# The expert down matrix read as four neighbouring rows per partition, with SwiGLU transposes that take every fourth column

## What is computed

```python
def moe_swiglu(h, w_router, w_gate, w_up, w_down):
    probs = jax.nn.softmax((h @ w_router).astype(jnp.float32), axis=-1)
    top_p, top_i = lax.top_k(probs, TOP_K)
    top_p = top_p / jnp.sum(top_p, axis=-1, keepdims=True)
    gates = jnp.sum(jax.nn.one_hot(top_i, N_EXPERTS, dtype=jnp.float32) * top_p[..., None], axis=-2)
    y = jnp.zeros(h.shape, jnp.float32)
    for e in range(N_EXPERTS):
        y = y + gates[..., e:e + 1] * swiglu(h, w_gate[e], w_up[e], w_down[e]).astype(jnp.float32)
    return y.astype(h.dtype)
```

## Time and profile before

| what | value |
|---|---|
| time, median of 3 runs | 1859.83 us (1857.74 to 1859.93) |
| the profiled execution, its time | 1861.72 us |
| the profiled execution, its span | 1860.0 us |
| PE busy | 1790.0 us, 96% of the span |
| DVE busy | 1168.1 us, 63% |
| ACT busy | 885.7 us, 48% |
| read from HBM | 429.82 MB |

### The profile page before, as it was taken

One profiled execution on the slowest core, in us unless ns is written; L12 is line 12 of the kernel. 1 busy time (PEld: TensorE's weight loads), 2 busy tenths in 40 slices (PEclk: granted clock), 3 DMA queues, 4 the chain that ended last, 5 costly groups with the idle time before them and its releaser, 6 DMA issues.

```text
span 1860.0 us, 27046 instructions
## 1 busy us (share of the span) xinstructions
PE 1790.0 (96%) x10718; PEld 1447.5 (78%) x10718; DVE 1168.1 (63%) x1128; ACT 885.7 (48%) x926; POOL 31.2 (2%) x93
## 2 busy tenths in 40 slices
PE   7989999999999999979999999999999999999997
PEld 6757788888767799658888878878788888788785
DVE  4660100000057674658988878888789888788885
ACT  2351110000014322256676667677666766676673
POOL 5000000000010000000000000000000000000000
PEclk9998999999999999979999999999999999999998
DMA  9201333334323100429999989999899999899992
GB/s 323 91 9 40 130 135 135 135 108 141 96 91 136 46 4 4 170 91 347 370 340 347 361 307 356 354 353 360 306 358 362 344 344 365 304 363 351 349 365 111
DMA packets 190894, 432.62 MB, mean 233 GB/s; under 512 B 9587, under 2 KB 10611, under 8 KB 190772
## 3 DMA queue, kind: packets, MB, share of 16 engines
q1 hardware_dynamic: 190384, 430.76, 64.1%
q10 hardware_dynamic: 388, 0.14, 0.0%
HBM read 429.82 MB, written 1.05 MB: 232 GB/s over the span
## 4 chain that ended last, share of the span: by engine, by line
PE 85%; DVE 8%; ACT 4%; issue 2%; ACTq 0%; DVEq 0%
PE ps L974 15%; PE ps L976 15%; PE ps L975 15%; PE ps L640 11%; PE ps L651 6%; PE ps L676 2%; PE ps L552 2%; PE ps L941 2%; PE ps L956 2%; PE ps L624 2%; DVE wsplit L1704 2%; PE ps L896 1%; PE ps L795 1%; PE ps L810 1%; PE ps L997 1%
## 5 line engine op out<-in xcount | busy, mean ns | idle before, releaser
L1704 DVE TENSOR_TENSOR wsplit<-raw_w,wsplit 128x2048 fp32r<-128x2048 f32 x336 | 749.8, 2284 | 68.4 <-ACT wsplit L1288 68.4
L1288 ACT ACTIVATE wsplit<-raw_w 128x2048 fp32r<-128x2048 f32 x336 | 624.1, 1914 | 63.8 <-PE ps L976 63.8
L974 PE MATMUL ps<-wsplit,xsplit 128*128 128x512 f32 x896 | 361.2, 403 | 8.7 <-DVE wsplit L1704 8.1
L976 PE MATMUL ps<-wsplit,xsplit 128*128 128x512 f32 x896 | 351.3, 392 | 0.0
L975 PE MATMUL ps<-wsplit,xsplit 128*128 128x512 f32 x896 | 350.9, 392 | 0.0
L640 PE MATMUL ps<-arena 128*128 128x272 f32 x896 | 208.8, 395 | 3.6 <-DVE arena L1352 3.6
L974 PEld LDWEIGHTS ps<-wsplit,xsplit 128*128 128x128 f32 x896 | 169.3, 189 | 47.9 <-DVE wsplit L1704 12.7
L640 PEld LDWEIGHTS ps<-arena 128*128 128x128 f32 x896 | 171.2, 191 | 41.1 <-issue 4.0
L976 PEld LDWEIGHTS ps<-wsplit,xsplit 128*128 128x128 f32 x896 | 169.4, 189 | 36.6
L975 PEld LDWEIGHTS ps<-wsplit,xsplit 128*128 128x128 f32 x896 | 169.8, 189 | 35.2 <-issue 1.9
L974 PE MATMUL ps<-wsplit,hsplit 128*128 128x512 f32 x448 | 179.6, 401 | 0.0
(11 more groups left out here) (305 smaller groups left out, 1657.2 us busy)
## 6 DMA issues: line engine op xcount, KB each, us to landing
raw_w<-in_moe_w_gate SPq DMA_DIRECT2D x114, 1024.0 KB, 6.5
raw_w<-in_moe_w_up SPq DMA_DIRECT2D x112, 1024.0 KB, 7.6
raw_w<-in_moe_w_down SPq DMA_DIRECT2D x112, 1024.0 KB, 6.9
arena<-in_ffn_w_gate SPq DMA_DIRECT2D x7, 2048.0 KB, 7.8
arena<-in_ffn_w_up SPq DMA_DIRECT2D x7, 2048.0 KB, 7.7
arena<-in_ffn_w_down SPq DMA_DIRECT2D x8, 1792.0 KB, 7.7
arena<-in_attn_w_qkv SPq DMA_DIRECT2D x3, 2048.0 KB, 12.7
arena<-in_attn_w_o SPq DMA_DIRECT2D x2, 2048.0 KB, 20.6
```

What stands on the lines that cost most here:

```text
L974: mm(o, x_[0], w_[0], start=first_, stop=False)
L976: return mm(o, x_[1], w_[0], start=False, stop=last_)
L1288: A(wsplit[:, m % NRING, 0, :], raw_w[:, m % NRAW, :], ACT.Copy).then_inc(w_hi, 1)
L1704: v.tensor_tensor(wsplit[:, m % NRING, 1, :], raw_w[:, m % NRAW, :], wsplit[:, m % NRING, 0, :].bitcast(F32), ALU.subtract).then_inc(w_lo, 1)
```

## The change

In L369 the split of the 512 rows of a down block changes from (k p) to (p k). Partition `p` now holds the four neighbouring rows `4 p` to `4 p + 3`, and chunk `k` holds row `4 p + k`. Half `h` of a down tile is the chunks `2 h` and `2 h + 1` as before, which are now the rows `4 p + 2 h` and `4 p + 2 h + 1`: for each partition 8192 bytes that lie in one piece in HBM. Before they were two pieces of 4096 bytes, 512 KB apart. The pieces of neighbouring partitions start 16384 bytes apart now; the rows between them are those of the other half. The issuing instruction changes its form from 128x2x1024 elements to 128x2048.

To match, the `k`-th transpose takes the columns `k`, `k + 4`, `k + 8` and so on of the 512 hidden columns: 128 words that lie 16 bytes apart in a partition, in place of 128 words in one piece. All else stays, instruction for instruction and in the same order on every engine: the writing side of the transposes, `hsplit`, the matmuls, the waits and the rings.

```diff
@@ -366,7 +366,7 @@
 
             we_g = moe_w_gate[0].rearrange("e (k p) n -> e p k n", p=P)
             we_u = moe_w_up[0].rearrange("e (k p) n -> e p k n", p=P)
-            we_d = moe_w_down[0].rearrange("e (f k p) n -> e f p k n", p=P, k=QB)
+            we_d = moe_w_down[0].rearrange("e (f p k) n -> e f p k n", p=P, k=QB)
 
             def expert_tiles(i, it, a, b):
 
@@ -994,7 +994,7 @@
                         if q in (0, XQ):
                             pe.wait_ge(xg_ev, tables * 2 + (2 if q == 0 else 4))
                         for k in range(QB):
-                            last = tr(ps[:, 4, k * P:(k + 1) * P], hbuf[:, q % 2, k * P:(k + 1) * P], ident[:, :])
+                            last = tr(ps[:, 4, k * P:(k + 1) * P], hbuf[:, q % 2, :].rearrange("p (i k) -> p k i", k=QB)[:, k, :], ident[:, :])
                         last.then_inc(et_mm, 1)
 
                     def down(q):
```

## The result

| | median us | lowest to highest | runs |
|---|---|---|---|
| before | 1859.95 | 1857.74 to 1864.69 | 14 |
| after | 1863.94 | 1858.44 to 1866.93 | 14 |

The ratio is 1.0023 with a 95% interval of 1.0014 to 1.0032: 4.3 us slower, 2.6 to 6.0. The time lies in the range of the prediction, 3.6 us above its likeliest value. The forecast was "no change", with a bound of 0.2%. The ratio lies on that bound and the interval reaches to both sides of it, so what can be said is: slower by a little, at or just past what the prediction still called no change. The median also lies 0.9 us above the range of 1857 to 1863 us that the prediction gave to its own forecast.

A forecast was written before the change was run, and what follows sets the result against it. The prediction took PE to bound the expert stage. DMAs 0, transposes 0 to 0.8 us and PE's waits unchanged gave 1861.7 to 1862.5 us profiled, 1860.3 us on the runs' scale; range 1856 to 1881 us for 8 in 10.

The forecast's parts named there:

- no change: Whole kernel: time within 0.2% (3.7 us) of before, likeliest 1860.3 us, own range 1857 to 1863; chance 0.55.
- What bounds the kernel: Expert stage: PE is the bound, holding 85% of the span; no engine is released by a weight half's landing.
- The down DMAs at zero: The 112 down DMAs: 8 KB pieces in place of 4 KB change the time by 0.
- their margin: Down halves: 17 us spare per turn, 0.6 us each, so hidden until one takes 3.3 us and not 2.7.
- The second rival: Down DMAs get slower and the DMA becomes the bound; at 3.6 us per half 34 us more, 1894 us; chance 0.05.
- The streaming side as the bound of a plain transpose: Transposes, L997: streaming the identity sets 107.5 of 109 ns; the load's 49 ns of reading is hidden, 60 ns to spare.
- f: Transposes' loads, L997: factor by which the 16-byte stride lengthens the reading part; costs little up to 2, loads bound above 2.2.
- the 111.6 ns that the prediction took from the gather: Pace of L941, whose load is 192 ns; taken as the most a transpose would need at a doubled reading part.
- The factor of the stride: Transposes, L997: the reading part grows at most twofold, so the 224 transposes cost 0 to 0.8 us.
- the marks that the prediction named: Load of L997 in the changed profile: 139 ns unchanged, up to 192 if reading doubles, above 220 the prediction is wrong.
- The first rival: Strided loads become the bound at L997 alone, three exposed per block: 7 us to 15 to 20 us slower; chance 0.34.
- Nobody amplifies it: Engines waiting for the transposes, mainly ACT (20.5 us): they lose nothing against PE, so the price is paid once, on PE.

## Why the prediction was right or wrong

**What bounds the kernel: right.** PE's stream is the bound, and nothing of the 8 KB pieces shows in the time: alone they gave 0.9997 (0.9989 to 1.0006).

**The down DMAs at zero: right, but their margin was mis-sized.** The prediction divided by a turn of 244 us. A turn is 255 us, by the first matmuls of two turns shown above (1078.17 and 1333.34). With 255 us the margin is 28 us per turn, 1.0 us per down half, and the point 3.7 us in place of 3.3. The run with 512 B pieces, at some 3.6 us, already cost PE 4.4 us at three places. So an average over the turn says roughly where the price begins, and not that nothing is paid before. The second rival was still weaker than I put it: the transfers did not get slower either, 6.9 us to landing against 7.0.

**The streaming side as the bound of a plain transpose: right.** The load went from 139 to 187 ns at a stride of 8 and the pace stayed at 109 ns. The point at which a strided load begins to cost, a reading of some 107 ns, f of 2.2, holds within a few ns. By the same sum the load at 8 has a reading of 97 ns and costs nothing. The load at 16 (196 ns) has 106 ns and a pace of some 112 ns, like the 111.6 ns that the prediction took from the gather.

**The factor of the stride: this step failed.** I took f up to 2. A strided load occupies 120 ns, against the 49 ns that I had worked out for the reading: f is about 2.4. The record says the same: 208 ns less 139 is 69 ns more, 118 ns of reading. It passes the 109 ns of the streaming side by 11 ns, and the term that was put at 0 to 0.8 us measured 2.4 us. My reason, that the streaming side takes 2.2 words per ns, was of words in one piece, as the text granted, and did not carry over. The load's record of 208 ns is just between the marks that the prediction named (192 for f = 2, 220 as the sign of error), and the block's 0.47 us just above "0.43 to 0.45".

**The first rival: right in mechanism and place, below its prices.** The strided load became the bound, at L997 alone. Three steps of a block are exposed, as many as it said, but they are the third and fourth transpose and the matmul behind them, 11 ns each, with some 10 ns more around them: 2.4 us and not 7 to 20. It had 0.34; it is what happened. That the forecast "no change" and the likeliest time came out so near all the same is owed to the small size of the excess, 11 ns, and not to the reason that was given for f.

**Nobody amplifies it: right.** ACT's wait for the transposes went from 20.5 to 21.2 us, and PE's waits did not change.

**The Trainium skill's rule.** "SBUF — State Buffer", section "Door 1: The DMA port swizzle", says that two hits on a 16-byte line are needed for full bandwidth. The load did slow, as the rule says. But a stride of 2 words has two words on each line and had the same 120 ns as 4, and a stride of 8 was cheaper than both. The measurements decide: the rule gives the sign here, but not which stride is cheap.

**What stays open.** The paces and the turns show 2.4 us. The medians say 4.3 (2.6 to 6.0), 3.5 (1.5 to 5.6) and, with the stride alone, 3.0 us (1.1 to 4.8). Two of the three intervals hold 2.4, and the first just misses it. The granted clock may carry the rest. Its mean was 0.9785 over the 29 runs of the kernel before, 0.9778 with the stride alone and 0.9773 with both, and among those 29 runs 0.001 less clock goes with some 1.2 us more. That would be 0.7 and 1.3 us, which with 2.4 gives 3.1 and 3.7 us. It is a relation between runs and no experiment. Whether the stride makes the falls of the clock more frequent, or whether the runs happened to lie that way, is not shown; the kernel in which DVE makes the order, without a strided load, had 0.9773 too.

## What to carry to other kernels

Before a DMA is improved, look whether any engine is released by its landing: here a DMA share of 0.95 left room for down halves to grow from 2.7 to 3.0 us at no price, and larger pieces gave nothing back. When a single time seems unchanged, compare the waits of PE and the granted clock as well: the 512 B pieces cost 4.4 us of waits that a better clock covered. Before an operand is given a stride, find out which side of the instruction sets its pace and how far the other is from it; a load that grows by 69 ns cost 11 ns, and one that grows by 48 cost nothing. A new order that is put into an access pattern adds no instruction, but can be paid by the engine that walks it, here by PE (2.4 us) or, when moved, by DVE and through it again by PE (2.8 us).

## What the runs showed of the hardware

- The load of a transpose of 128 x 128 float32 words takes 139 ns in one piece, 187 ns at a stride of 8 words, and 209 ns at 2 and 4 words. The price does not grow with the distance, and 6 words was the dearest of those tried (137 ns for a transpose, against 109 in one piece).
- DVE's product of 128 x 512 float32 took 679 ns written in one piece and 1105 ns with neighbouring words written 128 words apart and all operands walked as 128 x 4.
- DMA packets of 8 KB for a third of the traffic made the others' time to landing longer (gate 6.5 to 7.1 us, up 7.6 to 8.0 us), without a change in the total rate: 347 GB/s against 348.
- After a wait of 2.7 us on PE the granted clock fell to 0.50 for 3.4 us in some turns and stayed at 1.00 in others; a fall cost 1.6 us of a turn of 255 us.
